# Homes of two block products' weights and the places of sum steps, top-k rounds and remainders in a two-layer gated trunk

## The reference, cut to what matters

```python
h = rms_norm(x, norm_g[l])
proj = jnp.einsum('bsd,de->bse', h, w_in[l])
...
score = jnp.where(admissible[None], score, -jnp.inf)
_, idx = lax.top_k(score, topk)                    # topk = 128
...
o_a = jnp.einsum('bse,ed->bsd', y_a, w_oa[l])
o_b = jnp.einsum('bse,ed->bsd', y_b, w_ob[l])
merged = jax.nn.sigmoid(g_a + gate_b[l, 0]) * o_a + jax.nn.sigmoid(g_b + gate_b[l, 1]) * o_b
x = x + jnp.einsum('bsd,de->bse', merged, w_out[l])
```

## Time and profile before

| What | Value |
|---|---|
| median of 3 runs | 807.29 us (806.7 to 807.37) |
| the profiled execution | 807.44 us, its span 805.5 us |
| TensorE busy | 783.4 us (97%) |
| VectorE busy | 642.0 us (80%) |
| ScalarE busy | 382.7 us (48%) |
| granted TensorE clock, mean | 0.992 |

### The profile page before, as it was taken

The page is one execution under the profiler, slowest core; times in us unless marked ns, Lnnn a source line. Parts: engine busy times, 40 slices in busy tenths (PEclk is TensorE's granted clock), DMA queues, the critical chain, the costliest instruction groups (busy, mean ns, idle before and its releaser), DMA issues.

```text
span 805.5 us, 11491 instructions
## 1 busy us (share of the span) xinstructions
PE 783.4 (97%) x4124; PEld 671.6 (83%) x4124; DVE 642.0 (80%) x1078; ACT 382.7 (48%) x706; POOL 130.4 (16%) x117
## 2 busy tenths in 40 slices
PE   7999999999999989899999999999999998998998
PEld 7988888888888769888899888888888886898886
DVE  5779999978787876569986899998887778745895
ACT  6576643342344346644564765433335433547242
POOL 1157600000000103012211664000000001210130
PEclk9999999999999999999999999999999999999999
DMA  9644133312323238595873531333231314385674
GB/s 335 206 127 134 55 104 105 104 53 83 101 79 105 30 76 134 147 271 119 188 229 106 170 102 53 97 103 105 79 104 55 99 58 77 60 178 190 176 137 125
DMA packets 44841, 97.89 MB, mean 122 GB/s; under 512 B 3056, under 2 KB 3248, under 8 KB 44784
## 3 DMA queue, kind: packets, MB, share of 16 engines
q1 hardware_dynamic: 32320, 67.12, 26.5%
q0 software_dynamic: 12176, 29.45, 17.7%
q10 hardware_dynamic: 288, 0.59, 0.2%
HBM read 90.85 MB, written 6.29 MB: 121 GB/s over the span
## 4 chain that ended last, share of the span: by engine, by line
PE 88%; DVE 7%; issue 3%; ACT 1%; DMA 1%; DVEq 0%; ACTq 0%
PE bank L793 18%; PE bank L795 18%; PE bank L794 18%; PE bank L911 5%; PE bank L830 3%; PE bank L832 3%; PE bank L831 3%; PE bank L860 3%; PE bank L862 3%; PE bank L861 3%; PE bank L785 2%; PE bank L767 2%; PE bank L723 1%; PE bank L738 1%; PE bank L737 1%
## 5 line engine op out<-in xcount | busy, mean ns | idle before, releaser
L1338 DVE TENSOR_TENSOR w_lo<-w_raw,w_hi 128x1024 fp32r<-128x1024 f32 x144 | 186.5, 1311 | 19.7 <-ACT w_hi L996 16.0
L996 ACT ACTIVATE w_hi<-w_raw 128x1024 fp32r<-128x1024 f32 x144 | 148.3, 1056 | 38.0 <-DMA w_raw<-in_w_out 20.4
L793 PE MATMUL bank<-h_lo,w_hi 128*128 128x512 f32 x320 | 128.0, 400 | 0.0
L795 PE MATMUL bank<-h_hi,w_hi 128*128 128x512 f32 x320 | 124.8, 390 | 0.0
L794 PE MATMUL bank<-h_hi,w_lo 128*128 128x512 f32 x320 | 124.6, 389 | 0.0
L793 PE MATMUL bank<-w_lo,h_hi 128*128 128x512 f32 x256 | 100.5, 393 | 0.0
L795 PE MATMUL bank<-w_hi,h_hi 128*128 128x512 f32 x256 | 99.9, 390 | 0.0
L794 PE MATMUL bank<-w_hi,h_lo 128*128 128x512 f32 x256 | 99.8, 390 | 0.0
L672 POOL DMA_DIRECT2D w_raw<-in_w_in x16 | 19.5, 1232 | 421.8 <-DVE w_lo L1338 421.8
L795 PEld LDWEIGHTS bank<-h_hi,w_hi 128*128 128x128 f32 x320 | 60.0, 188 | 12.9
L794 PEld LDWEIGHTS bank<-h_hi,w_lo 128*128 128x128 f32 x320 | 60.2, 188 | 12.3
(11 more groups left out here) (201 smaller groups left out, 1724.2 us busy)
## 6 DMA issues: line engine op xcount, KB each, us to landing
w_raw<-in_w_in SPq DMA_DIRECT2D x92, 512.0 KB, 3.8
w_raw<-in_w_in POOLq DMA_DIRECT2D x16, 512.0 KB, 6.0
w_raw<-in_w_out POOLq DMA_DIRECT2D x16, 512.0 KB, 6.3
w_raw<-in_w_out SPq DMA_DIRECT2D x12, 512.0 KB, 7.0
out<-x_sb POOLq DMA_DIRECT2D x4, 1024.0 KB, 5.8
w_raw<-in_w_oa SPq DMA_DIRECT2D x8, 512.0 KB, 3.3
w_raw<-in_w_ob SPq DMA_DIRECT2D x8, 512.0 KB, 4.4
x_sb<-out POOLq DMA_DIRECT2D x2, 2048.0 KB, 13.6
```

Source lines behind the costliest of these rows:

```text
L793: nc.tensor.matmul(dst, s_h, m_l, start=(n == 0), stop=False)
L795: last = nc.tensor.matmul(dst, s_h, m_h, start=False, stop=(n == len(pairs) - 1))
L996: nc.scalar.activation(hi, w_raw[:, raw_slot(layer, u)], ACT.Copy).then_inc(s_whi.sem, 1)
L1338: nc.vector.tensor_tensor(lo, w_raw[:, raw_slot(layer, u)], hi.bitcast(F32), ALU.subtract) \
```

## The change

It gives gb a table of homes of its own. In it a22 lies in the upper half of region 1 (the second block's home, a12's), and s6 alone in the upper half of region 0. ob's weights are split: the units of its first two k blocks go to the lower half of region 1, the other two to the upper half of region 0. In out, a12 and s6 exchange upper halves, so that a22 again follows a12. The waits in `home` follow the new places. The ten sum steps all move into the ga slots, two each in GA2 and GA6. Three top-k rounds of the largest block move from slots 40 to 42 to slots 26, 30 and 31. The roundings and remainders of the sums get slots of their own, two of them in gb, and the tables of weight units are written anew.

```diff
-W_HOME = {"a11": (0, 0), "a12": (0, 1), "s5": (1, 0), "s6": (1, 1), "s3": (0, 0), "s4": (1, 0), "a22": (1, 1)}
+W_HOME = {"a11": (0, 0), "a12": (1, 1), "s5": (1, 0), "s6": (0, 1), "s3": (0, 0), "s4": (1, 0), "a22": (1, 1)}
...
-H_ROUNDED = ["s5", "s4", "s3", "s6"]
-REGION = [0, 1, 0, 1, 0, 1, 0, 1, 0, 1, 0, 1, 1, 0]
-
-LATE_GATE_UNITS = dict(scalar=[0, 0, 1, 1, 4, 5, 6, 7, 8, 9], vector=[0, 1, 2, 2, 4, 5, 6, 7, 9, 9])
-OB_UNITS = dict(scalar=[10, 10, 11, 12], vector=[10, 11, 12, 13])
+H_ROUNDED = ["s5", "s3", "s6", "s4"]
+GATE_HOME = {"a11": (1, 0), "a12": (1, 1), "s5": (0, 0), "s6": (0, 1), "s3": (1, 0), "s4": (0, 0), "a22": (1, 1)}
+
+GATE_UNITS = dict(scalar=[0, 1, 3, 5], vector=[1, 2, 5, 7])
+LATE_GATE_UNITS = dict(scalar=[0, 0, 2, 2, 3, 4, 6, 7, 8, 8], vector=[0, 1, 2, 3, 4, 5, 7, 7, 8, 9])
+OB_UNITS = dict(scalar=[9, 9, 10, 11], vector=[10, 10, 11, 12])
...
+H_STEPS = {JOB_GA[0]: [0], JOB_GA[1]: [1], JOB_GA[2]: [2, 3], JOB_GA[3]: [4], JOB_GA[4]: [5], JOB_GA[5]: [6],
+           JOB_GA[6]: [7, 8], JOB_GA[7]: [9]}
+H_HI_AFTER = {JOB_OA[1]: "s5", JOB_OA[5]: "s3", JOB_GB[2]: "s6", JOB_GB[3]: "s4"}
+H_LO_AFTER = {JOB_OA[3]: "s5", JOB_GB[0]: "s3", JOB_GB[3]: "s6", JOB_GB[5]: "s4"}
...
-              23: [(2, 1), (3, 2)], 28: [(3, 2)], 29: [(3, 1)], **{s: [(3, 1)] for s in range(32, 43)}}
+              23: [(2, 1), (3, 2)], 26: [(3, 1)], 28: [(3, 2)], 29: [(3, 1)], **{s: [(3, 1)] for s in range(30, 40)}}
...
+        def ob_weights(k):
+
+            return (w_hi1[:], w_lo1[:]) if k < 2 else (w_hi0[:], w_lo0[:])
...
-            region, upper = W_HOME[name]
+            region, upper = (W_HOME if g == OUT_G else GATE_HOME)[name]
             k = slice(HALF_K * upper, HALF_K * upper + HALF_K)
-            return ((w_hi1, w_lo1) if region != REGION[g] else (w_hi0, w_lo0)), k
+            return ((w_hi1, w_lo1) if region else (w_hi0, w_lo0)), k
...
             g, i = unit_of(u)
+            if g == GB_G + 1:
+                used = gate_job("s3" if i < 2 else "s6", 1) + 1
+                return [w[:, 2 * i:2 * i + 2] for w in ob_weights(i)], s_job.at(layer, used)
...
-            used = dict(a11=FIRST_JOB[g - 1], a12=FIRST_JOB[g - 1], s5=FIRST_JOB[g], s6=FIRST_JOB[g],
-                        s3=that("a11", 1) + 1, s4=that("s5", 1) + 1, a22=that("s6", 1) + 1)[name]
+            used = dict(a11=gate_job("s4", 1) + 1 if g == OUT_G else FIRST_JOB[g - 1], a12=FIRST_JOB[g - 1],
+                        s5=FIRST_JOB[g], s6=FIRST_JOB[g], s3=that("a11", 1) + 1, s4=that("s5", 1) + 1,
+                        a22=that("a12", 1) + 1)[name]
...
+            if g == GB_G - 1:
+                return [GB_U + i for i, job in enumerate(GATE_UNITS[engine]) if job == j - JOB_OA[0]]
...
-                if n in JOB_OA[1::2]:
-                    h_sum_rounded(layer, H_ROUNDED[(n - JOB_OA[1]) // 2])
+                if n in H_HI_AFTER:
+                    h_sum_rounded(layer, H_HI_AFTER[n])
...
-                    if n in JOB_GA + JOB_OA[:2]:
-                        h_sum_step(layer, n - JOB_GA[0])
-                    if n in JOB_OA[2::2]:
-                        h_sum_remainder(layer, H_ROUNDED[(n - JOB_OA[2]) // 2])
-                    if n == JOB_GB[0]:
-                        h_sum_remainder(layer, "s6")
+                    for step in H_STEPS.get(n, []):
+                        h_sum_step(layer, step)
+                    if n in H_LO_AFTER:
+                        h_sum_remainder(layer, H_LO_AFTER[n])
```

More of the change, by code:

```diff
@@ L452, in weights @@
                 return index_hi[:, :, 0:W512], index_lo[:, :, 0:W512]
-            return (w_hi1[:], w_lo1[:]) if REGION[g] else (w_hi0[:], w_lo0[:])
+            return (w_hi1[:], w_lo1[:]) if g % 2 else (w_hi0[:], w_lo0[:])
+        def ob_weights(k):
+            return (w_hi1[:], w_lo1[:]) if k < 2 else (w_hi0[:], w_lo0[:])
         def slot_free(layer, g):
-            if g == GB_G + 1:
-                return s_job.at(layer, gate_job("s3", 1) + 1)
             if g >= 2:
@@ L868, in job @@
                 n = FIRST_JOB[g] + j
-                w_hi, w_lo = weights(g)
+                if name != "ob":
+                    w_hi, w_lo = weights(g)
                 b = bank_of(n)
@@ L878, in job @@
                     for k in range(A_GROUPS):
+                        if name == "ob":
+                            w_hi, w_lo = ob_weights(k)
                         c = slice((j % 4) * P, (j % 4 + 1) * P)
```

## The result

The changed kernel took 789.03 us in the median (788.23 to 789.69, 4 runs) beside 807.33 for the kernel before in the same comparison; the ratio is 0.9769, its 95% interval 0.9748 to 0.9789. That is 18.3 us less. Predicted were 789.5, with 787.4 to 794.5 as the range.

The account below looks back on a forecast made before the run. The prediction took TensorE to bound the kernel: 20.0 us to be had, less 1.8 (part 3) and 0.4 (part 2), gave 17.8 off 807.44, so 789.6 profiled and 789.5 in the median, range 787.4 to 794.5.

Parts of the forecast that it names:

- What can be had: TensorE's waits in oa and gb, the delays they hide and the half clock: 20.0 us over both layers.
- Part 1: In oa, 9.8 us of VectorE's work leaves, 17.5 us stays, and TensorE's waits there vanish.
- Part 2: End of gb: a22's new home ends the 2.90 us wait at GB12; 0.2 us of delay per layer remains.
- rival (a): The hand-over in gb stays a wait: 798.6 us from about 2.9 us late, 792 if milder; chance 0.15.
- Rival (d): The change does nothing, as VectorE's lateness merely moves from oa into gb: 807 us; chance 0.04.
- The loads: POOL loads in gb land in time: median 5.9 us, at most 13.0, the tightest 3 us ahead of ScalarE's need.
- Rival (c): Late load landings in gb hold ScalarE and the s4 add, GB12 about 8 us late: 808.5 us; chance 0.03.
- Part 3: Price in zb and za: the slot 26 round holds TensorE 0.9 us at ZA3's end per layer, 1.8 us.
- Part 4: Exchange of halves in out, ob's earlier first units and the reload of x cost nothing.
- The sum: Over the whole kernel, 17.8 us less than the profiled execution's 807.44: 789.6 us.

Follow-up runs that it names:

- e4: The changed kernel with the top-k round of slot 26 moved to slot 24: 786.98 us.
- e6: The changed kernel with the three top-k rounds back in slots 40 to 42, sums still spread: 787.60 us.
- e7: The changed kernel with sum steps, roundings and remainders of the sums back in their old slots: 789.75 us.
- e1: The changed kernel with one wait put back, a22's units again waiting for s6's last job: 801.30 us.
- e3: The kernel before with top-k rounds, sum steps, roundings and remainders of the sums in the new slots, homes and unit tables old: 798.04 us.
- e5: The changed kernel with the remainder of one more ob unit ahead of the add of s4 in GB10's slot: 790.24 us.
- e8: e4 with ob's first two remainders behind the add of s4 and its third one slot later: 787.09 us.
- e9: The changed kernel with the top-k round of slot 30 in slot 29, ahead of the first scaling: 792.71 us.
- e2: The changed kernel with only new homes and unit tables; top-k rounds, sum steps, roundings and remainders of sums in old slots: 798.92 us.

## Why the prediction was right, point by point

**What can be had, 20.0.** oa and gb now run in 76.00 us per layer, and e4, without any wait, also needs 76.00: 9.92 + 10.66 = 20.6 us were there. The term was 0.6 too small; it was added up from idle times and estimates for what they hide. One reading in it was incomplete: the clock was at half not in three stretches but in four. The fourth lies at the kernel's start, 12.3 to 15.7 us, where the change reaches nothing, so the term stands.

**Part 1.** Right: no wait in oa. The view of stretches of the kernel after, the one from oa's start over 29.1 us:

```profile
263.50:292.60 29.10, 29.10 (x144) 23.79 (x142) 20.20 (x39) 11.43 (x19) 2.49 (x2) 1.00 0.33 60
```

VectorE is busy for 20.20 of 29.10 us. The 17.5 worked out were 2.7 too low, and the timelines show 2.2 of it. VectorE, late in the kernel before, did the last bank product of oa only behind that stretch's end, and all but 0.1 us of the third remainder of a sum too, so that one remainder less than counted could leave the stretch (1.1 us), and one bank product comes in (0.7, now at 291.12):

```profile
294.88 1.23 DVE L1498 SCALAR_TENSOR_TENSOR hs<-h_raw,hs 128x1024 fp32r<-128x1024 f32 x1 [0.24 <-DVE g_a L1559]
296.02 0.68 DVE L1559 SCALAR_TENSOR_TENSOR g_a<-g_a,bank 128x512 f32<-128x512 f32 x1
```

And the pass that closes the block of top-k (0.4) did not leave: in the changed kernel it still lies in oa.

```profile
267.76 0.43 DVE L1427 TENSOR_SCALAR score<-score 128x512 f32<-128x512 f32 x1
```

Part of the other 0.5 us is that the 9.8 us were counted from start to start, pauses between instructions included, while the 27.29 they were taken from is busy time alone. The mistake cost nothing, since 20.20 still leaves 8.9 us. e6 and e7 show what the working did not say: half of the relief was enough for all but 0.6 to 0.8 us per layer.

**Part 2.** Right, and shown by e1 and e3. The add of s4 was worked out to reach TensorE 11.3 us after GB8's start. GB12 starts 11.46 us after GB8, so by the rows above it was 11.07. Margin 0.15 by the working, 0.4 in the trace: so narrow that rival (a), a hand-over that stays a wait, was near, and e5 shows what 1.14 us more would have cost. The 0.2 us taken per layer for weight loads was the one wrong term; e8 shows it at nothing. Rival (d), that the lateness only moves into gb, did not come true: no wait of TensorE is left in gb.

**The loads.** No POOL load delayed ScalarE in oa and gb of the changed kernel. Its POOL loads in layer 0:

```profile
L686 POOL DMA_DIRECT2D w_raw<-in_w_in x8: 1194/1205/1309, 272.1 to 314.7; - x8
...
DMA to landing us min/median/max: 5.8/5.9/7.3
```

The landing times of the earlier trace rows are those of all loads of w_raw in that stretch, SyncE's too, and the prediction read them as those of the POOL loads. For the POOL loads alone they were 5.6/6.0/9.7 before: the median is the same, and the 13.0 us belong to another queue's load. The issues are as short as in the earlier trace rows, though VectorE now works beside them with fewer pauses. The lock of the shared port by which the Trainium skill (SBUF — State Buffer, SBUF: two separate sides) lets such loads wait does not show here with this mix of VectorE's operations. Whether any of them runs in a mode that would take the lock, no run shows.

Rival (c) spoke of ob's units, which SyncE's queue loads. Its mechanism is there, only small. In the changed kernel the third of them held ScalarE:

```profile
330.10 1.06 ACT L1013 ACTIVATE w_hi<-w_raw 128x1024 fp32r<-128x1024 f32 x1 [0.38 <-DMA w_raw<-in_w_ob]
```

There it cost TensorE nothing. The longest such wait is 1.24 us (third unit again, e4, layer 0), also without a cost; 0.21 us at the second unit took about a quarter of a microsecond of e5's margin. The 8 us that the rival needed are far from any of these.

**Part 3.** Right to a few hundredths: 0.9 us per layer expected, 0.89 and 0.92 measured, in the place that was named. VectorE and TensorE there, after:

```profile
186.28 0.69 DVE L1558 SCALAR_TENSOR_TENSOR z_b<-t_half,bank 128x512 f32<-128x512 f32 x1
187.21 0.69 DVE L1558 SCALAR_TENSOR_TENSOR z_b<-t_half,bank 128x512 f32<-128x512 f32 x1 [0.24 <-DVE z_b L1558]
...
211.60 0.29 DVE L1434 TENSOR_SCALAR probs<-probs,row_inv 128x128 f32<-128x128 f32 x1
```

```profile
211.95 0.33 PE L790 MATMUL bank<-eye,probs 128*128 128x128 f32 x1 [0.72 <-DVE probs L1434]
```

The wait of 0.81 us for ScalarE of the earlier trace rows has become a link of 0.24, and the scaling is what TensorE waits for. e4 and e9 take the price away and raise it. The second scaling and the ga slots cost nothing, as worked out.

**Part 4.** Right: the part from ob to the end is 59.64 us in both, and that from ob to the next layer's scores differs by 0.2 us.

**The sum.** 17.8 us expected for the profiled execution, 17.75 measured (807.44 to 789.69). That is closer than the terms deserve, and luck: 20.6 - 1.8 + 0.2 would have been 19.0, and 1.3 us at the start took the difference. Of the eleven profiles of this case nine reached the first scores after 203.6 to 204.4 us, the changed kernel and e9 after 205.35 and 205.37. These two are also the only ones in which the clock was at half from 25 to 28.4 us. The same stretch in the kernel before and after, with the granted clock as the third number from the end:

```profile
25.00:28.40 3.40, 3.30 (x26) 3.09 (x26) 3.36 (x7) 1.41 (x4) 0.00 (x0) 1.00 0.55 184
25.00:28.40 3.40, 3.35 (x14) 3.37 (x15) 3.37 (x7) 0.73 (x2) 0.18 (x1) 0.50 0.62 201
```

TensorE did 14 matmuls in place of 26, and from there on the changed kernel stays 1.3 us behind up to the first scores. The program up to there is the same as before, and e1 and e4 to e8, which begin with the same program, have no such stretch. So nothing ties it to the change; what brings it on stays open. The first matmul of ob, expected at about 338.4 in layer 0, came at 339.56, late by little but this. The changed kernel's four runs fit the same reading: 788.23 and 788.41 us at a mean granted clock of 1.000, 789.65 and 789.69 at 0.998. Between e4 and the changed kernel's medians, 2.05 us, the parts explain 1.84.

## What to carry to other kernels

Where one engine is the bound and others feed it, list its waits, work the feeding engine's slots out one by one against the time the fed engine would need without a stall, and do the same at the places that the work moves to: here that gave both the gain and the price of 0.9 us, and e4 shows that the price was a choice of slot. A buffer's home is a wait: in an engine that works strictly in order, an early place in its program with a late release holds everything behind it, so choose the home by which release comes first. When a stage lacks a few us, half of a planned relief can be enough; try each half, since the rest is free to stay where it costs nothing.

## What the runs showed that I had not expected

Half the clock does not follow every delay, and when it does its length varies. A delay of 3.0 to 3.1 us (2.8 to 2.9 of idle time) was followed by a stretch at half clock in three of four cases in the kernel before; in e2, with a wait of 2.8 us in each layer, it followed in the first layer alone. Its stretches of 3.4 us behind the two waits, with the granted clock as the third number from the end:

```profile
286.00:289.40 3.40, 2.97 (x7) 1.83 (x8) 3.16 (x4) 2.19 (x3) 0.00 (x0) 0.50 0.00 0
676.40:679.80 3.40, 3.40 (x15) 2.54 (x16) 3.16 (x4) 1.71 (x3) 0.00 (x0) 1.00 0.00 0
```

TensorE did 7 matmuls in the one and 15 in the other; oa and gb took 81.81 and 81.27 us there. The two delays of 2.4 us in e9 were followed by none: the part to oa grew by no more than the delay. In e3 one stretch at half clock went on twice as long, over 6.8 us, though TensorE had work in it:

```profile
724.30:731.10 6.80, 6.04 (x28) 6.05 (x29) 5.42 (x7) 4.49 (x9) 0.78 (x1) 0.50 0.76 234
```

That is the layer in which oa and gb took 81.78 us, against 80.49 in the other, with the same wait of 2.9 us. So the same stall cost 4.5 us in one layer and 5.8 in the other. e1 had a stretch of this length too, in layer 1 behind its wait of 4.6 us (725.8 to 732.6). And the start of the kernel, whose program is the same in all of these up to slot 24, varies by up to 1.8 us (203.61 to 205.37), 1.3 of it by the stretch at half clock shown above and as much in all as this change gives back in za: differences of that size are read from parts of the trace, not from the total.
